# Gated linear attention heads 1 to 3: strips projected in 18 pairs by seven block products, weight sums made by accumulating DMA

## The reference, cut to what matters

```python
proj = rmsnorm(h, norm_g) @ w_in          # 528 x 1024 by 1024 x 6160
q, k, v, g_low, r = jnp.split(proj, [o1, o2, o3, o4], axis=-1)
log_a = jax.nn.log_sigmoid((g_low @ w_gate_up + b_gate)) / GLA_GATE_NORMALIZER
q = q.reshape(B, L, GLA_HEADS, GLA_HEAD_K) * (GLA_HEAD_K ** -0.5)   # 256 a head, v: 512
o = gla_chunked(q, k, v, log_a)
o = rmsnorm(o, head_norm_g).reshape(B, L, D_INNER)
return h + (o * jax.nn.silu(r)) @ w_out
```

## Time and profile before

| what | value |
|---|---|
| timed runs, median of 3 | 1005.32 us (1005.11 to 1005.88) |
| profiled execution, span from first to last instruction | 1002.4 us |
| TensorE busy | 994.3 us, 99% |
| VectorE busy | 732.4 us, 73% |
| ScalarE busy | 552.2 us, 55% |
| GpSimd busy | 90.6 us, 9% |
| bytes moved | 107.69 MB, mean 107 GB/s |

### The profile page before, as it was taken

How to read it: one execution, slowest core, us unless ns; L and a number is a source line. 1 busy time by engine, 2 the same in 40 slices (tenths; PEclk the granted TensorE clock), 3 DMA queues, 4 the chain that set the end, 5 groups by cost and what they waited for, 6 DMA issues and landing times.

```text
span 1002.4 us, 19364 instructions
## 1 busy us (share of the span) xinstructions
PE 994.3 (99%) x7843; PEld 940.7 (94%) x7843; DVE 732.4 (73%) x1190; ACT 552.2 (55%) x915; POOL 90.6 (9%) x97
## 2 busy tenths in 40 slices
PE   9999999999999999999999999999999999999998
PEld 8999999999999999998889989999899989988897
DVE  6874677477567875435889976898589966989875
ACT  6754654564465554334566655656366645566633
POOL 0000000000000000000232211222112211210000
PEclk9999999999999999999999999999999999999999
DMA  8221231132122113333334432444244533486332
GB/s 293 78 71 64 67 101 45 63 103 68 64 72 97 44 63 127 105 108 104 113 82 122 108 137 60 134 103 137 89 114 110 120 117 91 124 257 233 115 106 84
DMA packets 42392, 107.69 MB, mean 107 GB/s; under 512 B 4784, under 2 KB 12848, under 8 KB 42304
## 3 DMA queue, kind: packets, MB, share of 16 engines
q1 hardware_dynamic: 41584, 105.78, 34.6%
q10 hardware_dynamic: 720, 0.68, 0.2%
HBM read 98.34 MB, written 7.90 MB: 106 GB/s over the span
## 4 chain that ended last, share of the span: by engine, by line
PE 89%; DVE 6%; ACT 2%; issue 2%; DMA 0%; DVEq 0%; ACTq 0%
PE psum L2076 50%; PE psum L2452 13%; PE psum L2371 7%; PE psum L2430 3%; PE psum L2566 3%; PE psum L2201 2%; DVE w_lo L1226 1%; PE psum L2411 1%; PE psum L2149 1%; PE psum L2573 1%; PE psum L2197 1%; PE psum L2399 1%; PE psum L2398 1%; PE psum L2400 1%; PE psum L2170 1%
## 5 line engine op out<-in xcount | busy, mean ns | idle before, releaser
L1226 DVE TENSOR_TENSOR w_lo<-raw,w_hi 128x1024 fp32r<-128x1024 f32 x156 | 191.5, 1242 | 38.3 <-ACT w_hi L682 28.0
L682 ACT ACTIVATE w_hi<-raw 128x1024 fp32r<-128x1024 f32 x156 | 162.9, 1052 | 47.8 <-PE psum L2371 29.5
L2076 PE MATMUL psum<-xh,w_hi 128*128 128x264 f32 x768 | 159.1, 288 | 0.2 <-DVE w_lo L1240 0.2
L2076 PE MATMUL psum<-xl,w_hi 128*128 128x264 f32 x768 | 155.9, 285 | 0.0
L2076 PE MATMUL psum<-xh,w_lo 128*128 128x264 f32 x768 | 155.2, 283 | 0.0
L2076 PEld LDWEIGHTS psum<-xh,w_hi 128*128 128x128 f32 x768 | 118.6, 189 | 1.6 <-issue 1.4
L2076 PEld LDWEIGHTS psum<-xl,w_hi 128*128 128x128 f32 x768 | 119.5, 188 | 0.0
L2076 PEld LDWEIGHTS psum<-xh,w_lo 128*128 128x128 f32 x768 | 119.1, 189 | 0.0
L624 POOL TENSOR_TENSOR sub<-sub,cst 128x128 f32<-128x128 f32 x64 | 50.8, 796 | 650.1 <-DMA sub<-sums 649.8
L2076 PE MATMUL psum<-y_lo,w_hi 128*128 128x264 f32 (+2 forms) x336 | 79.6, 299 | 0.0
L2452 PE MATMUL psum<-y_lo,w_hi 128*128 128x256 f32 x312 | 57.9, 287 | 0.1
(11 more groups left out here) (353 smaller groups left out, 2486.5 us busy)
## 6 DMA issues: line engine op xcount, KB each, us to landing
raw<-w_all SPq DMA_DIRECT2D x143, 512.0 KB, 3.5
sub<-sums SPq DMA_DIRECT2D x16, 264.0 KB, 7.2
y_keep<-sq SPq DMA_DIRECT2D x14, 256.0 KB, 2.2
y<-y_keep SPq DMA_DIRECT2D x14, 256.0 KB, 6.5
sub<-sums SPq DMA_DIRECT2D x16, 200.0 KB, 6.3
yr<-y_keep SPq DMA_DIRECT2D x12, 256.0 KB, 4.9
sub<-sums SPq DMA_DIRECT2D x16, 136.0 KB, 4.9
hT<-xT SPq DMA_DIRECT2D x8, 264.0 KB, 5.3
```

Source lines behind the costliest of these rows:

```text
L682: nc.scalar.activation(w_hi[:, n % HI_RING, :], raw[:, n % LO_RING, :], ACT.Copy).then_inc(hi_made, 1)
L1226: nc.vector.tensor_tensor(w_lo[:, n % LO_RING, :], raw[:, n % LO_RING, :], w_hi[:, n % HI_RING, :].bitcast(F32), ALU.subtract).then_inc(lo ...
L2076: i = nc.tensor.matmul(o, w[a][:, k % KT, :], x[b][:, k, c0:c1], start=k == first and a == b == 0, stop=k == last and a == 1)
```

## The change

Heads 1 to 3 of GLA have 36 strips. The change computes them in 18 pairs. A pair is two strips a and b of one kind; its weights and tokens are split into 2 x 2 blocks, the features in two halves of 4 k tiles and the tokens in two halves of 264 columns, and the result (two strips by two token halves) comes from seven products instead of eight (Winograd's form of Strassen's scheme). Each product is 4 k tiles x 3 parts = 12 matmuls of 264 columns (`gp`). The pairs of a head are called q, k, v, r (R0, R1), w (V2, V3) and s (R2, R3), and are numbered 0 to 17 over the three heads.

- **Token sums.** The tokens are normalised in place (`norm_tokens`, eight instructions), four sums of blocks are made from them (`token_sum`), and blocks and sums are split again into high and low parts (`tokens_high`, `tokens_low`, `token_sums_high`, `token_sums_low`). Some of these overwrite `xh`, `xl` and `hT`, so they come behind R03, the last strip of head 0, and `hT` is loaded again during the output projection. The multiplication by `rstd` at the strips' read-out goes away, for the gate logits too, and the query scale moves into the epsilon of the head norm.
- **Weight sums.** With w11, w12 the halves of a's weights and w21, w22 those of b's: s1 = w21 + w22, s2 = s1 + w11, s3 = w21 + w11, s4 = s2 + w12. SP loads one term, and an accumulating transfer that POOL issues adds the other. Four of these a pair. s2 and s4 lie in the slot e of the raw ring, s3 in place of w21, s1 in one of three buffers by turns (`s1_even`, the memory of `rstd`, a row of `y`). POOL issues second, next pair's first, third and fourth sum in this order.
- **Outputs.** ScalarE copies the products 1, 6 and 7, which accumulate in one bank, after each of the three (`keep`), and VectorE adds a copy and a product's bank for each of four output quarters (`pair_out`).
- **Order.** TensorE runs for pair n product 1, then product 3 of pair n - 1, then 2, 6, 5, 7, 4 of pair n. Head 0 keeps its strips, in another order towards its end; output A{h}3 of a head is made in the next head's pair q.

```diff
+GP = [(x, h) for h in range(1, GLA_HEADS) for x in "qkvrws"]
+GP_STRIPS = {"q": ("Q", 0, 1), "k": ("K", 0, 1), "v": ("V", 1, 0), "r": ("R", 1, 0), "w": ("V", 3, 2), "s": ("R", 3, 2)}
+GP_BANK = {1: 2, 6: 2, 7: 2, 2: 3, 5: 0, 3: 0, 4: 1}
+for _n in range(len(GP)):
+    GP_ORDER += [(1, _n)] + ([(3, _n - 1)] if _n else []) + [(p, _n) for p in (2, 6, 5, 7, 4)]
...
+            def load_s1(n):
+                if n == 1:
+                    sp.wait_ge(strip_made, 8)
+                    sp.wait_ge(xn_made, KT)
+                elif n == 2:
+                    sp.wait_ge(xl_made, KT + 7)
+                elif n > 2:
+                    sp.wait_ge(prod_done, GP_AT[(5, n - 3)])
+                if n:
+                    sp.wait_ge(s1_sum, 16 * n)
+                sp.dma_start(gs1(n)[0], w_all[AT[f"p{n:02d}b"], :, 0:CH // 2]).then_inc(s1_loaded, 16)
...
+            def load_pair(n):
+                load(CHUNK[f"p{n:02d}a"])
+                load_s2(n)
...
+                load(CHUNK[f"p{n:02d}b"])
+                load_s4(n)
...
+            def fourth_sum(n):
+                pool.wait_ge(s4_loaded, 16 * (n + 1))
+                pool.wait_ge(s2_sum, 16 * (n + 1))
+                pool.dma_start(pair_raw(n, "e")[1], pair_raw(n, "e")[0], accum_op=ALU.add).then_inc(s4_sum, 16)
...
+            def keep(n, i):
+                act.wait_ge(prod_done, GP_AT[((1, 6, 7)[i], n)])
...
+                nc.scalar.activation((u1, u2, u3[:])[i], bank(GP_BANK[1], 0, HALF), ACT.Copy, scale=(1.0, 1.0, -1.0)[i]).then_inc(copied, 1)
...
+            def second_low(n):
+                dve.wait_ge(s1hi_made, 2 * n + (2 if n else 1))
+                dve.wait_ge(s4_sum, 16 * (n + 1))
...
+            def pair_out(n, name):
...
+                product, u, i = {"11": (2, u1, 0), "22": (5, u3[:], 2), "21": (4, u3[:], 2), "12": (3, u2, 1)}[name]
...
+                tt(to, u, bank(GP_BANK[product], 0, HALF), ALU.subtract if name == "22" else ALU.add, out_made)
...
+            def gp(product, n):
+                w = pair_weights(n, product)
...
+                for k in range(KT // 2):
+                    for a, b in PARTS:
+                        i = nc.tensor.matmul(o, w[k][a], x[b][:, k, :], start=product not in (3, 6, 7) and k == a == b == 0,
```

More of the change, by code:

```diff
@@ L175, in loaded @@
 def loaded(c):
[L176 removed]
+    return c[0] != "e" and not (c[0] == "s" and c[2] in "456") and not (c[0] == "p" and c[3] == "e")
 LOADED = [c for c in CHUNKS if loaded(c)]
@@ L261, in program @@
         acc = sb("acc", [P, T])
-        rstd = sb("rstd", [P, T])
+        with ExitStack() as one:
+            rstd = sb("rstd", [P, T], F32, one)
+        rstd_lo = sb("rstd_lo", [P, T], F32R)
         rtok = sb("rtok", [P, NBLK + 1])
@@ L885, in _ @@
+                if h + 1 < GLA_HEADS:
+                    gate_exp(h + 1)
+                else:
+                    y_high(0)
+                n = pair("s", h)
                 gla_square(h, 0)
                 gla_values_hi(h, 1)
-                ahead(f"R{h}2")
+                second_high(n)
+                keep(n, 0)
+                if h + 1 < GLA_HEADS:
+                    gate_log(h + 1)
+                pair_high(n, "b")
+                pair_high(n, "e")
+                pair_high(n + 1, "a")
@@ new lines, in _ @@
+                    gla_mask(0)
+                    gla_scores_lo(0)
+                    ahead("V02")
+                    for k in range(KT // 2, KT - 1):
+                        norm_tokens(k)
+                    gate_min(1, 0)
+                    norm_tokens(KT - 1)
+                    gate_min(1, 1)
+                    token_sum(0)
+                    token_sum(2)
+                    token_sum(1)
+                    gla_out(0, 0)
+                    token_sums_low(1, 0, 1, th[:, 1], 3, 0)
@@ new lines, in gla_transposed, with pair_weights @@
+                if h + 1 == GLA_HEADS and v == 1:
+                    pe.wait_ge(glo_made, 5 * h + 5)
+                transposed(f"X{h}{v}", gvt2[v % 2])
+            def pair_weights(n, product):
+                if product == 5:
+                    pe.wait_ge(s1lo_made, n + 1)
+                    low = gs1(n)[1]
+                    return [(gs1_hi[:, k // 2, k % 2 * P:(k % 2 + 1) * P], low[:, k * P:(k + 1) * P]) for k in range(KT // 2)]
+                x, half = {1: ("a", 0), 2: ("a", 1), 6: ("e", 0), 3: ("e", 1), 7: ("b", 0), 4: ("b", 1)}[product]
+                m = CHUNK[f"p{n:02d}{x}"]
+                if product == 1:
+                    pe.wait_ge(half_lo, 2 * n + 2)
+                elif product == 6:
+                    pe.wait_ge(half_lo, 2 * n + 3)
+                else:
+                    pe.wait_ge(lo_made, m + 1)
+                c = slice(half * CH // 2, (half + 1) * CH // 2)
+                hi, low = four(w_hi[:, m % HI_RING, c]), four(w_lo[:, m % LO_RING, c])
+                return [(hi[:, k, :], low[:, k, :]) for k in range(KT // 2)]
```

1019 lines of the change are left out of this document (797 added, 222 removed).

## The result

| kernel | median of runs, us | lowest to highest | against before, 95% interval |
|---|---|---|---|
| before, 11 runs | 1004.96 | 1004.31 to 1005.88 | |
| changed, 11 runs | 1011.05 | 1006.93 to 1015.13 | 1.0055 [1.0038, 1.0072] |

The forecast was 991.8 us. The time lies just above the range (980 to 1010), on the side of rival C. (The ratios of this document are those of the means, so they differ a little from what the medians give.) The changed kernel's runs also lie 8 us apart, those of before 1.6. Its profiled execution was its fastest, 1006.93 us with a span of 1005.1. So the two traces, 2.7 us apart in span, show less than half of the 6.1 us between the medians.

The account below looks back on a forecast made before the run. TensorE, busy 994.3 of 1002.4 us, was taken as the bound. 24.6 - 4.5 - 3.6 - 3.0 = 13.5 us saved; 1002.4 - 13.5 = 988.9 span, + 2.9 = 991.8 us, range for 8 in 10: 980 to 1010.

Parts of the forecast that it names:

- rival C: DMA engines become the bound in the pairs once an accumulate takes over 2.27 us; at 2.4, 1014.6 us; chance 0.20.
- In DMA time an accumulate costs 0.8 us if it moves like a load: DMA-made weight sums in each pair: 0.8 us of DMA time per accumulate, upper end 2.4.
- it is hidden, cost nothing: Tightest chain of weight sums, load to split: 7.6 us against eight products' 11.8, so no cost.
- rival B: The DMA-made weight sums land late, at 6.5 us each: 10.8 us lost, 1002.6 us; chance 0.15.
- TensorE's saving: Heads 1 to 3: 1728 matmuls become 1512 at 122.8 ns, 210.3 to 185.7 us, saving 24.6 us.
- The handover: From head 0 to the pairs: VectorE's work of 21.2 us against TensorE's 16.7, a wait of 4.5 us.
- some 5 us before VectorE comes to them: At the handover, the second pair's first sum and second half of weights land some 5 us before VectorE needs them.
- Each pair: Waits at ScalarE's copies in pair w and late values in pair s: 1.2 us a head, 3.6 us in all.
- Head 3: Four copies of y ahead of A32's square and values: 2.5 + 0.5 = 3.0 us of wait.
- VectorE's and ScalarE's loads: Busy time per head: VectorE 68.8 us (87%), ScalarE 58.5 us (74%); neither is the bound by its sum.

Follow-up runs that it names:

- plain copies: The changed kernel with its 72 accumulating transfers made plain copies of the same size, sources and queue, leaving out the weight sums: 993.09 us.
- short sums: The changed kernel with each of its 72 accumulating transfers cut from 512 to 16 columns a row: 992.57 us.
- m1: Transfers of 256 KB alone, without the kernel, one by one, then eight at once: DMA time 0.69 to 0.79 us plain, 1.53 and 1.67 accumulating.
- four further copies: The kernel with plain copies, plus four 256 KB copies a pair issued by ScalarE that nothing waits for: 1004.31 us.
- five: The kernel with plain copies, plus five 256 KB copies a pair on ScalarE's queue that nothing waits for: 1008.97 us.
- half sums: The changed kernel with each accumulating transfer cut to 256 of 512 columns: 996.13 us.

## Why the prediction was wrong, step by step

**What failed: "In DMA time an accumulate costs 0.8 us if it moves like a load", and "it is hidden, cost nothing".** It measured 1.58 us here and 1.53 to 1.67 alone. I had the right argument in rival C ("two reads are twice 0.8 us, 1.6") and used it to argue C away, since its bound was t = 2.27. That bound took the DMA engines as a bucket that may be filled to the brim: 18 x (5.5 + 4 x 1.58) = 213 us of 262. The demand does not come evenly: loads start when a product frees a slot, and each sum waits for a load. At a mean share of 0.83 the time has risen by 11 us already, with stretches at 0.97; up to 0.71 it had risen by 0 to 3. Landing went with it, from the 3.5 us that I took to medians of 4.3 to 6.5 us for POOL's transfers, which is rival B's picture (waits on w_lo that lead back to DMA) with C's cause. B's price for 6.5 us each was 10.8; 18.5 were lost.

**TensorE's saving, 24.6 us: right, a little high.** Busy time of the product's line and of the strip's line before, in one head each ('plain copies', then before; PE, PEld, clock, DMA share, GB/s):

```profile
148.43:229.64 81.21, 63.73 (x504) 62.01 (x504) 1.00 0.65 216
```

```profile
193.84:281.34 87.50, 71.67 (x578) 70.52 (x578) 1.00 0.22 73
```

126.4 ns a matmul against 124.0 by the same view. In long pieces of the chain a product's matmul is 121.7 ns (20.45 us for 168), no slower than a strip's before; between other work it is up to 133 (3.19 for 24). 576 x 0.1240 - 63.73 = 7.7 us a head, 23.1 in all. I had taken the pitch from one piece of the second layer that lies between other products, and applied it to all.

**The handover, 4.5 us: right in size.** In 'plain copies' TensorE waits there 2.5 us on w_lo, 1.5 on ScalarE's copy, 0.9 on gsr: 4.9. So 3.4 of it is waited for on VectorE, where my sum had all of it; TensorE's own wait for ScalarE was in no term. In the changed kernel the third pair's first sum can't be loaded until the new low tokens are made (110.37 in the chain), and POOL's queue stands behind it, so another 6.0 us go: the scores of head 1 begin at 154.44, and at 148.43 in 'plain copies'. Of the second pair the first sum and the loads did land in time, by 106.4 us; its fourth sum, which my sentence ("some 5 us before VectorE comes to them") left out, landed at 119.4, and VectorE waited 1.3 us for it. The third pair I had not looked at.

**Each pair, 1.2 us a head: right in size, by luck.** TensorE stands still 81.2 - 79.9 = 1.3 us a head in 'plain copies', but not where I had put it: over two heads it waits 0.9 us at the gate logits and 0.7 at the transposes, both for VectorE's read of the gate logits (s), 0.6 at the outputs and 0.3 on w_lo, and never for ScalarE's copy of a product. Starts of the scores of heads 1 to 3 in the changed kernel, by its chain:

```profile
154.44 3.10 PE psum L2775 x16
241.91 3.10 PE psum L2775 x16
325.47 3.10 PE psum L2775 x16
```

In 'plain copies' they begin at 148.43, 229.64 and 310.79: 81.2 us a head, against 87.50 and 80.5 forecast. In the changed kernel a head lasts 87.47 and 83.56. Over plain copies that is 6.0, 6.3 and 2.4 us in the three stretches, 14.7 in all, and nothing behind 325 us.

**Head 3, 3.0 us: too much.** From the last scores to the output projection 'plain copies' has TensorE busy 46.3 of 47.5 us: 1.1 us, 0.9 of it a wait on the head's sums of squares. The projection's first 24 matmuls stand in the gap.

**Sum.** 13.5 us were forecast, 12.3 are there with the short sums (1004.9 - 992.6), and with the full ones 18.5 more are lost (1011.05 - 992.57). The 12.3 are 23.1 less some 8.5 of waits (4.9, 2.5 and 1.1) and a rest of about 2.3, of which the clock's 0.98 before the first scores makes 1.7 by my estimate (0.02 x 83). The **clock** was in no term: in the changed kernel TensorE ran 4.9 us longer for the same matmuls than with plain copies, in stretches where it had gaps and was granted 0.89 to 0.96. **VectorE's and ScalarE's loads** came near: 70.4 and 57.4 us a head in 'plain copies' (68.8 and 58.5 forecast).

## What to carry to other kernels

Work moved to DMA has a price in DMA time, not only in landing: add up the engines' time per stage, count an accumulating transfer double, and leave room where transfers start from each other's semaphores (here a mean share of 0.71 cost 0 to 3 us, 0.76 up to 6 and 0.83 about 11). If a term of the sum is seen in no row, let the bound that is argued (two reads, twice the time) into the forecast, not only into a rival. To tell full engines from a full queue, add transfers nobody waits for, on a queue that nobody else needs.

## What was not expected of the hardware

- An accumulating transfer of 256 KB takes 1.53 to 1.67 us of the 16 engines (plain 0.69 to 0.79) with nothing else running, from memory and within SBUF alike, 1.58 in the kernel (plain 0.73), and 0.87 us of POOL to issue (plain 0.54 to 0.57).
- Eight accumulates at once: POOL issued three, then stood 5.66 us before the fourth (in other places of `m1` after one or two already). Eight plain ones: six, then 5.35 us.
- 36 additions of 128x512 on POOL made VectorE 26 us busier in all, 72 made it 49 us busier; the groups with an input in PSUM kept their time.
- Kernels with a high DMA share spread between runs: 8 us the changed kernel, 6.6 with four further copies, 5.0 with five, 1.1 with short sums. The share alone does not tell: half sums spread by 7.7 us at 0.68, the fourth sum on VectorE (`v4`) by 1.3 at 0.75.
